# Moving the first score tiles one piece earlier and two pieces of the next stage between the last attention steps

## The reference

```python
q, k, v, u, gate_a, gate_s = jnp.split(h @ w_in, IN_SPLITS, axis=-1)
for g, (window, dilation) in enumerate(ATTN_GROUPS):      # (128,1) (512,4) (2048,16)
    o, l = dilated_window_attention(q[g], k[g], v[g], slopes[g], window, dilation)
attn = jnp.sum(softmax(lses)[..., None] * outs, axis=0)
y = jax.nn.gelu(s5_ssm(u, ...))
merged = sigmoid(gate_a) * (attn @ w_attn_up) + sigmoid(gate_s) * ((y @ w_glu_v) * sigmoid(y @ w_glu_g))
x = x + rms_norm(merged @ w_out, norm_mix_post)
```

## Time and profile before

| what | value |
|---|---|
| time, median of 3 runs | 2892.91 us (2892.59 to 2898.84) |
| the profiled execution: its own time / its span | 2893.86 us / 2892.1 us |
| TensorE busy | 2800.1 us, 97% of the span |
| VectorE / ScalarE / GpSimd busy | 975.3 / 753.8 / 376.6 us |
| chain of work that ended last | TensorE 94%, VectorE 2%, DMA 2%, ScalarE 1%, GpSimd 1% |
| attention stage of pair 0, scores(2) to first qkv piece of pair 1 | 357.98 to 386.03 us |
| attention stage of pair 1, same borders | 598.81 to 626.86 us |

### The profile page before, as it was taken

How to read it: one execution, slowest core, us unless ns; L and a number is a source line. 1 busy time by engine, 2 the same in 40 slices (tenths; PEclk the granted TensorE clock), 3 DMA queues, 4 the chain that set the end, 5 groups by cost and what they waited for, 6 DMA issues and landing times.

```text
span 2892.1 us, 34686 instructions
## 1 busy us (share of the span) xinstructions
PE 2800.1 (97%) x13805; PEld 2337.2 (81%) x13805; DVE 975.3 (34%) x1044; ACT 753.8 (26%) x828; POOL 376.6 (13%) x578
## 2 busy tenths in 40 slices
PE   4999999999999999999799999999999999999997
PEld 3788878887888888888588888888888888888886
DVE  4223332232322232332523233332324233332426
ACT  3222232231422222322422222222222222222223
POOL 7729107760000000000100000000000000000000
PEclk9999999999999999999899999999999999999999
DMA  5534553335233233343133233333333333333332
GB/s 132 155 122 134 120 124 99 97 80 142 88 95 101 94 94 101 95 167 98 63 101 98 92 101 95 94 102 94 99 97 94 94 102 94 94 99 97 94 95 101
DMA packets 249053, 299.23 MB, mean 103 GB/s; under 512 B 20864, under 2 KB 210368, under 8 KB 248096
## 3 DMA queue, kind: packets, MB, share of 16 engines
q1 hardware_dynamic: 230888, 264.83, 30.0%
q0 software_dynamic: 6864, 26.68, 3.8%
q10 hardware_dynamic: 11240, 6.85, 0.8%
HBM read 282.14 MB, written 16.19 MB: 103 GB/s over the span
## 4 chain that ended last, share of the span: by engine, by line
PE 94%; DVE 2%; DMA 2%; ACT 1%; POOL 1%; issue 0%; ACTq 0%; DVEq 0%
PE ps L309 21%; PE ps L310 21%; PE ps L311 21%; PE ps L348 7%; PE ps L347 7%; PE ps L346 7%; PE ps L327 2%; PE ps L331 2%; PE ps L329 2%; DMA h_r<-h_d 1%; DMA prm<-in_ssm_log_dt 1%; PE ps L529 1%; POOL t_q L1450 1%; PE ps L496 0%; PE ps L518 0%
## 5 line engine op out<-in xcount | busy, mean ns | idle before, releaser
L297 DVE TENSOR_TENSOR w_lo<-raw,w_hi 128x1024 fp32r<-128x1024 f32 x488 | 615.0, 1260 | 1517.5 <-ACT w_hi L293 1517.2
L309 PE MATMUL ps<-a_hi,w_hi 128*128 128x512 f32 x2432 | 949.5, 390 | 2.7 <-ACT u_st L821 1.2
L310 PE MATMUL ps<-a_lo,w_hi 128*128 128x512 f32 x2432 | 946.4, 389 | 0.0
L311 PE MATMUL ps<-a_hi,w_lo 128*128 128x512 f32 x2432 | 946.3, 389 | 0.0
L293 ACT ACTIVATE w_hi<-raw 128x1024 fp32r<-128x1024 f32 x488 | 516.7, 1059 | 1593.4 <-PE ps L311 1043.7
L309 PEld LDWEIGHTS ps<-a_hi,w_hi 128*128 128x128 f32 x2432 | 456.5, 188 | 101.3 <-DVE w_lo L297 2.9
L311 PEld LDWEIGHTS ps<-a_hi,w_lo 128*128 128x128 f32 x2432 | 456.5, 188 | 95.2
L310 PEld LDWEIGHTS ps<-a_lo,w_hi 128*128 128x128 f32 x2432 | 456.6, 188 | 93.5
L346 PE MATMUL ps<-w_hi,f_hi 128*128 128x512 f32 x704 | 273.9, 389 | 0.0
L347 PE MATMUL ps<-w_lo,f_hi 128*128 128x512 f32 x704 | 273.9, 389 | 0.0
L348 PE MATMUL ps<-w_hi,f_lo 128*128 128x512 f32 x704 | 273.9, 389 | 0.0
(11 more groups left out here) (213 smaller groups left out, 1981.5 us busy)
## 6 DMA issues: line engine op xcount, KB each, us to landing
raw<-in_w_in SPq DMA_DIRECT2D x152, 512.0 KB, 3.5
raw<-in_w_ffn_gate SPq DMA_DIRECT2D x88, 512.0 KB, 3.5
raw<-in_w_ffn_up SPq DMA_DIRECT2D x88, 512.0 KB, 3.5
raw<-in_w_ffn_down SPq DMA_DIRECT2D x88, 512.0 KB, 3.7
raw<-in_w_out SPq DMA_DIRECT2D x32, 512.0 KB, 3.7
raw<-in_w_glu_v SPq DMA_DIRECT2D x16, 512.0 KB, 3.5
raw<-in_w_glu_g SPq DMA_DIRECT2D x16, 512.0 KB, 3.6
h_d<-hc POOLq DMA_DIRECT2D x8, 576.0 KB, 3.4
```

What stands on the lines that cost most here:

```text
L297: nc.vector.tensor_tensor(w_lo[:, m % 2, :], raw[:, m % 4, :], w_hi[:, m % 2, :].bitcast(F32), ALU.subtract).then_inc(lo_ready, 1)
L309: nc.tensor.matmul(o, wh[:, k, cols], x_hi[:, kt0 + k, :], start=first and k == 0, stop=False)
L310: nc.tensor.matmul(o, wh[:, k, cols], x_lo[:, kt0 + k, :], start=False, stop=False)
L311: mm = nc.tensor.matmul(o, wl[:, k, cols], x_hi[:, kt0 + k, :], start=False, stop=last and k == 3)
```

## The change

Two things are moved, on all three engines; no work is added or taken away.

1. Tiles 0 and 1 are scored after pieces 8 and 9 of the last qkv stage (numbers from 0) and not after 9 and 10; VectorE takes their scores at its steps 10 and 11 and both norms at 12; ScalarE's two exps stand at its steps 11 and 12.
2. Pieces 0 and 1 of what follows the attention stage (qkv of pair 1, or the gates) are multiplied inside it: piece 0 after heads(5), piece 1 after heads(6), and heads(7) after that. The split of piece 1 moves into step t = 5 on ScalarE and VectorE, that of piece 2 into step t = 9. (Piece 0 is split in the qkv stage, as before.)

```diff
         def pe_first_scores(pe, pr, k):
-            if k in (9, 10):
-                pe_scores(pe, pr, k - 9)
+            if k in (8, 9):
+                pe_scores(pe, pr, k - 8)
@@ pe_attention, end of step t
                     mm.then_inc(heads, 1)
+                if t == 8:
+                    pe.wait_ge(biased, n0 + 8)
+                if t in (8, 9):
+                    next_piece(t - 8)
@@ act_first_exps
-            if k == 12:
-                act_exp(act, pr, 0)
-                act_exp(act, pr, 1)
+            if k in (11, 12):
+                act_exp(act, pr, k - 11)
@@ act_attention, end of step t
+                if t in (5, 9):
+                    split_hi(act, next_m + (1 if t == 5 else 2), 0)
@@ dve_first_scores
-                if k == 11:
-                    dve_scores(pr, 0)
+                if k in (10, 11):
+                    dve_scores(pr, k - 10)
                 if k == 12:
-                    dve_scores(pr, 1)
                     dve_norm(pr, 0)
+                    dve_norm(pr, 1)
@@ dve_attention
-                    if t < 9:
+                    if 3 <= t < 9:
                         dve_norm(pr, t - 1)
...
+                    if t in (5, 9):
+                        split_lo(dve, next_m + (1 if t == 5 else 2), 0)
```

More of the change, by code:

```diff
@@ L467, in pe_tables, with pe_qkv @@
                 (pe_lags, pe_inputs_turned)[(k - 1) % 2](pe, 4 * half + (k - 1) // 2)
-        def pe_qkv(pe, pr, g, between=None):
-            for k in range(12):
+        def pe_qkv(pe, pr, g, between=None, ks=range(12)):
+            for k in ks:
                 m, quads, kt0, first, last = B_QKV[pr] + k, 3 * g, 4 * (k % 4), k % 4 == 0, k % 4 == 3
@@ L501, in pe_first_scores, with pe_attention @@
         def pe_first_scores(pe, pr, k):
-            if k in (9, 10):
-                pe_scores(pe, pr, k - 9)
-        def pe_attention(pe, pr):
+            if k in (8, 9):
+                pe_scores(pe, pr, k - 8)
+        def pe_attention(pe, pr, next_piece):
             n0 = 8 * pr
@@ L621, in _ @@
             pe.wait_ge(g_copied, 8)
-            pe_attention(pe, 0)
-            pe_qkv(pe, 1, 0, lambda k: pe_chunk_inputs(pe, k - 2) if 2 <= k < 2 + OCT else None)
+            pe_attention(pe, 0, lambda k: pe_qkv(pe, 1, 0, ks=(k,)))
+            pe_qkv(pe, 1, 0, lambda k: pe_chunk_inputs(pe, k - 2) if 2 <= k < 2 + OCT else None, range(2, 12))
             pe_qkv(pe, 1, 1)
@@ L627, in _, with pe_g0 @@
             pe.wait_ge(s_copied, OCT)
-            pe_attention(pe, 1)
-            pe.wait_ge(biased, 16)
+            def pe_g0(k):
+                piece_f(pe, B_G0 + k, 0, k // 4, a_hi, a_lo, 4 * (k % 4), k % 4 == 0, k % 4 == 3)
+            pe_attention(pe, 1, pe_g0)
             for k in range(8):
-                piece_f(pe, B_G0 + k, 0, k // 4, a_hi, a_lo, 4 * (k % 4), k % 4 == 0, k % 4 == 3)
+                if k >= 2:
+                    pe_g0(k)
                 if k >= 2:
@@ L741, in act_tables, with act_qkv @@
                                   ).then_inc(k_stored, 16)
-        def act_qkv(act, pr, g, after=None):
-            for k in range(1, 13):
+        def act_qkv(act, pr, g, after=None, ks=range(1, 13)):
+            for k in ks:
                 split_hi(act, B_QKV[pr] + k, 3 * g)
@@ L760, in act_first_exps, with act_attention @@
         def act_first_exps(act, pr, k):
-            if k == 12:
-                act_exp(act, pr, 0)
-                act_exp(act, pr, 1)
-        def act_attention(act, pr):
+            if k in (11, 12):
+                act_exp(act, pr, k - 11)
+        def act_attention(act, pr, next_m):
             n0 = 8 * pr
@@ L838, in _ @@
             act_qkv(act, 0, 2, lambda k: (act_tables(act, 1, k), act_first_exps(act, 0, k)))
-            act_attention(act, 0)
-            with act.Fori(0, GROUPS - 1) as g:
-                act_qkv(act, 1, g)
+            act_attention(act, 0, B_QKV[1])
+            act_qkv(act, 1, 0, ks=range(3, 13))
+            act_qkv(act, 1, 1)
             act_qkv(act, 1, 2, lambda k: act_first_exps(act, 1, k))
-            act_attention(act, 1)
-            for k in range(1, 9):
+            act_attention(act, 1, B_G0)
+            for k in range(3, 9):
                 split_hi(act, B_G0 + k, 0)
@@ L993, in dve_tables, with dve_qkv @@
                     tt(st[:, :, 0:CH], st[:, :, 0:CH], d_blk[:, i:i + 3:2, :], ALU.add).then_inc(k_copied, 1)
-            def dve_qkv(pr, g, between=None):
-                for k in range(1, 13):
+            def dve_qkv(pr, g, between=None, ks=range(1, 13)):
+                for k in ks:
                     split_lo(dve, B_QKV[pr] + k, 3 * g)
@@ L1034, in dve_first_scores, with dve_attention @@
             def dve_first_scores(pr, k):
-                if k == 11:
-                    dve_scores(pr, 0)
+                if k in (10, 11):
+                    dve_scores(pr, k - 10)
                 if k == 12:
-                    dve_scores(pr, 1)
                     dve_norm(pr, 0)
-            def dve_attention(pr):
+                    dve_norm(pr, 1)
+            def dve_attention(pr, next_m):
                 n0 = 8 * pr
@@ L1128, in _ @@
             dve_qkv(0, 2, lambda k: (dve_tables(1, k), dve_first_scores(0, k)))
-            dve_attention(0)
+            dve_attention(0, B_QKV[1])
             def dve_chunk_inputs(b):
@@ L1137, in dve_chunk_inputs @@
                                       ps[:, 6 + b % 2, :].rearrange("p (a n) -> p a n", n=NCH)).then_inc(s_copied, 1)
-            dve_qkv(1, 0, lambda k: dve_chunk_inputs(k - 3) if 3 <= k < 3 + OCT else None)
+            dve_qkv(1, 0, lambda k: dve_chunk_inputs(k - 3) if 3 <= k < 3 + OCT else None, range(3, 13))
             dve_qkv(1, 1)
             dve_qkv(1, 2, lambda k: dve_first_scores(1, k))
-            dve_attention(1)
+            dve_attention(1, B_G0)
             def dve_outputs(b):
```

## The result

The changed kernel takes 2907.64 us (median of 6 runs, 2902.53 to 2908.87), the kernel before 2893.42 (6 runs). The ratio is 1.0044, 95% interval 1.0033 to 1.0055: 12.7 us slower, between 9.5 and 15.9. It compares all runs and not the two medians, which lie 14.2 us apart; the spans of the two profiled executions lie 13.3 apart. The forecast was 12.5 us slower, 2905.4, range 2900.4 to 2909.

What follows compares the result with a forecast made beforehand. From heads(7) of pair 1 to outputs(3), GpSimd's queue of table loads, not matmuls, sets the time. Pair 0 +2.2 and pair 1 13.0 - 2.2 - 0.5 = +10.3 give +12.5 us: 2905.4, range 2900.4 to 2909.

Steps and rivals of the forecast that it cites:

- Rival D: Table loads do not hang on heads(7) of pair 1; only the stages count, 2 x 2.2: 2897.3 us; chance 0.05.
- T: End of heads(7), the attention stage's last heads step; in pair 1 forecast 13.0 us later, with the table loads behind it.
- Part 1: Tiles 0 and 1 scored one piece earlier: 0 us for both stages, bounds 0 and minus 1.37 per stage.
- Part 2a: Split of piece 1 at step 5, mid-stage: scores(6) and TensorE 2.00 us later, bounds 0 and 2.24.
- Parts 2b and 2c: Pieces inside the stage cover a 0.30 us stall before heads(7); switching between kinds of work adds 0.47 us.
- P0: First piece of work after the attention stage, placed after heads(5); a piece between other work was priced at 5.67 us.
- the sum for pair 0: Up to chunk inputs(0): 2.00 - 0.30 + 0.47 = +2.2 us, if the g_r load is there in time.
- The new stall: TensorE at outputs(0) of pair 1 waits 11.4 us for the first t_q, where it waited 0.29.
- The reliefs: Pair 1, outputs(3): clock stays up, minus 2.2 us; then fewer competing weight loads, minus 0.5.
- Rival C: No relief: clock at half again at outputs(3), queue no faster: 2908.1 us, 0.7 more with late g_r; chance 0.17.
- Rival A: Weight queue silent during the outputs(0) stall, so the last h_r comes 3.5 us sooner: 2902.4 us; chance 0.12.

Runs made afterwards that it cites:

- pair 0 only: Changed kernel with pair 1 as before: pieces and splits moved in pair 0 only, the tiles in both; 2895.22 us, ratio 1.0003.
- the early tables: t_q 2 and 3 loaded before the wait for the last tile: on the changed kernel 2900.05 us (1.0019), on the kernel before 2893.61 us (1.0000).
- one piece inside: Changed kernel with only piece 0 inside each attention stage, piece 1 after heads(7), splits as in the change; 2896.77 us, ratio 1.0012.
- early tiles: Kernel before with only tiles 0 and 1 scored one piece earlier, after pieces 8 and 9; 2892.70 us, ratio 0.9996.
- split late: Kernel before with only the split of piece 1 moved to step 9 on ScalarE and VectorE; 2891.23 us, ratio 0.9991.
- pieces and splits alone: Changed kernel with the earlier scoring of tiles 0 and 1 undone, only pieces and splits moved; 2906.94 us, ratio 1.0041.
- split alone: Kernel before with only the split of piece 1 moved to step 5 on ScalarE and VectorE; 2896.48 us, ratio 1.0011.

## Why the prediction was right, step by step

**What bounds the kernel.** Right. The chain, the run for pair 0 only (0.9 us) and the early tables (about 7 us back in the changed kernel) all put the loss behind heads(7) of pair 1. Rival D would have left the time at 2897.3; it falls. The one step too strong was that the stretch from T to outputs(3) is a constant: it was 48.3 us in the changed kernel, 43.7 with one piece inside, and 46.6 in the run of the early tiles, where nothing behind T differs from before.

**Part 1.** Right: no gain that could be told, and the waits at transposes(1) stayed at 1.37 us.

**Part 2a.** Right. 2.00 us forecast. Transposes(6) of pair 0 came at 382.69, against 380.37, less the 0.44 that the stage began late: 1.88. TensorE took it one step sooner than the prediction had it, before transposes(5). ScalarE's part began 0.16 after `at_hi` and not 0.27, the rest was as priced (1.09 and 1.14).

**Parts 2b and 2c.** The wait behind the pieces is as described: transposes(6) still waited 1.38 and 1.39 us. A piece between other work was priced at 5.67 us from one that stands before outputs. Inside the stage P0 took 632.58 - 627.03 = 5.55, and heads(5) gave way to it after 1.26 us and not 1.34. So the sum for pair 0 was 404.55 - 402.57 - 0.44 = 1.54 us (chunk inputs(0) start at 404.55 in the trace of the changed kernel) where 2.2 stood, and T of pair 1 moved, from the start of its own shift, by 14.44 - 1.98 = 12.46 us where 13.0 stood.

**The new stall.** 11.4 us forecast, 11.01 measured, and the clock at half when it ended, swallowed by the wait behind it, as said: outputs(0) took 4.55 us (658.01 to 662.56).

**The reliefs.** Here the sum was wrong. The second, 0.5 us, was 0.8 in this trace: the last `h_r` at T + 48.3 and not 49.1. That is less than the 2.5 us by which traces of one queue differ, so whether there was such a relief is open. The first, the clock at outputs(3), was to give 2.2 us and gave nothing. I took it that a wait of up to 4.2 us leaves the clock up. It was 4.13 us, and in windows of the changed kernel (us, busy by engine, granted clock in the seventh column, DMA share, GB/s)

```profile
684.00:688.00 4.00, 1.47 (x7) 0.89 (x5) 0.00 (x0) 1.06 (x1) 0.00 (x0) 1.00 1.03 241
688.00:690.00 2.00, 0.40 (x4) 0.40 (x6) 0.00 (x0) 0.00 (x0) 0.00 (x0) 0.70 1.06 303
690.00:692.00 2.00, 2.00 (x22) 1.67 (x20) 0.00 (x0) 0.00 (x0) 0.00 (x0) 0.50 1.04 297
```

the clock fell to half within the last part of the wait, and outputs(3) with the piece after them took 701.01 - 689.60 = 11.41 us, against 10.81 before: 0.6 more, not 2.2 less. Pair 1 thus gave 12.46 - 0.8 + 0.6 = 12.2 us and not 10.3, and pair 0 gave 1.5 and not 2.2: 13.8 in place of 12.5. The misses are each under 3 us and of both signs, so that the total fits better than its parts is in part luck: the mechanism (T, the queue behind it, the new stall) was right, the clock relief was not. Rival C (clock at half again, queue no faster, 2908.1) describes the clock rightly. The time does not decide between the two: the median, 2907.64, is nearer to C, the 12.7 us of the ratio are nearer to the forecast's 12.5 than to C's 15.2, and the interval holds both.

**Rival A.** The weight queue fell silent in the stall, and the last `h_r` came 0.8 us sooner, not 3.5. The rate during it, 8 us from T + 12 (q0 is the tables' queue):

```profile
q0 software_dynamic: 450, 1.36, 104.9%
```

is 0.170 MB per us alone, against 0.143 alone and 0.144 shared before, and 0.24 alone with one piece inside (0.95 MB in 4 us). So "no faster alone" rested on one window of a rate that changes along the queue. In the 30 us from T + 14, weight loads moved 1.43 MB before and 0.62 in the changed kernel, and the tables' queue moved 4.34 and 4.40 MB: what the weight loads left free brought the tables next to nothing. The engines' time did go over to the tables' queue, 76.1% before and 89.3% in the changed kernel. That far the trace agrees with the rule on turns that I cited from the Trainium skill ("DMA: Bandwidth & Descriptors", section "Queues, rings and completion order"). The bytes did not follow the time, and why is open.

## What to carry to other kernels

Before work is put between the last instructions of a stage, look who is released by them: here one 1.3 us heads step releases 6 MB of loads, and 11 us ahead of it cost 12, though no wait shows there in the trace of before. A filler belongs in front of the wait that it is to cover, and its preparation (here a split on two engines) outside the ring that sets the pace. Where a queue of transfers is the bound, ask of each transfer which memory it waits for: in the kernel before, one of four tables moved ahead of the rest gave 9 us, and two moved gave nothing, because the first one needed then stood behind them.

## What the runs showed of the hardware

Clock: each wait of TensorE at outputs(3), of 3.4 to 7.5 us in eight kernels, cost speed behind it. Without a wait, outputs(4) starts 8.59 us after outputs(3). How much longer it took, by the timelines:

| kernel | wait before outputs(3), us | outputs(3) to (4), us | more than 8.59, us |
|---|---|---|---|
| split late | 3.40 | 11.17 | 2.6 |
| pieces and splits alone | 3.75 | 10.24 | 1.7 |
| changed | 4.13 | 11.41 | 2.8 |
| early tiles | 4.24 | 10.24 | 1.7 |
| one piece inside | 4.60 | 11.19 | 2.6 |
| before | 6.42 | 10.81 | 2.2 |
| pair 0 only | 6.85 | 10.94 | 2.4 |
| split alone | 7.51 | 10.90 | 2.3 |

The price does not grow with the wait. In the run of pieces and splits alone the granted clock was still 1.00 through the last full 2 us of the wait, and 0.50 from 692 to 694, behind it. The wait of 2.11 us at outputs(0) with one piece inside cost nothing: the next outputs came 8.59 us later.

Spread: the five kernels in which TensorE does not wait for the last `h_r` have runs that lie close together (2883.1 to 2885.0, 2882.0 to 2883.8, 2883.4 to 2889.3, 2898.7 to 2901.7, 2892.4 to 2896.6 us). The others spread by 6 to 14 us (before, 21 runs: 2887.8 to 2900.3). That the landing of the last `h_r` makes this spread fits the traces and is not shown by them, since one execution of each kernel was traced.

Queues: a weight load on SP's queue that began 2.8 us after heads(7), beside the first table loads, held 61% of the engines' time for 4 us, and the tables' queue moved 0.42 MB in them where it moved 0.95 without. In the 30 us from 641 of the kernel before, weight loads held 30% and the tables' rate was 0.144 MB per us. The tables' queue by itself moved 0.14, 0.17 and 0.24 MB per us in three stretches, each time with the engines at 99 to 105%. So these runs give no single rate for it, and no single price for a weight load beside it.
